# One level of Strassen in the up projections of four feed-forward stages of an eight-block FP32 model

## What is computed

```python
def _swiglu(x, wg, wu, wd):
    return (jax.nn.silu(x @ wg) * (x @ wu)) @ wd
```

## Time and profile before

| what | value |
|---|---|
| time, median of 3 runs | 3176.98 us (3176.74 to 3179.26) |
| the profiled execution's own time | 3175.48 us |
| its span, first to last instruction | 3173.7 us |
| TensorE busy | 3018.4 us, 95% of the span |
| VectorE, ScalarE, GpSimd busy | 1592.3, 1208.5, 527.0 us |
| stage `up3` in the trace | 1909.6 to 2150.3 us |

### The profile page before, as it was taken

How to read it: one execution, slowest core, us unless ns; L and a number is a source line. 1 busy time by engine, 2 the same in 40 slices (tenths; PEclk the granted TensorE clock), 3 DMA queues, 4 the chain that set the end, 5 groups by cost and what they waited for, 6 DMA issues and landing times.

```text
span 3173.7 us, 37430 instructions
## 1 busy us (share of the span) xinstructions
PE 3018.4 (95%) x13606; PEld 2468.7 (78%) x13606; DVE 1592.3 (50%) x1835; ACT 1208.5 (38%) x1599; POOL 527.0 (17%) x517
## 2 busy tenths in 40 slices
PE   7999988889999999799999879999999998999998
PEld 6888876768788887588888668888888886788886
DVE  6665356388566634633337844333433336843323
ACT  5553252258555423422223233222322224732221
POOL 1111010235311111211101111111111102611110
PEclk9999999889999999899999999999999999999999
DMA  4222332100123222222232112322332232222222
GB/s 160 105 93 77 105 124 69 53 14 1 54 93 104 82 91 92 75 105 93 82 103 82 54 40 93 104 86 91 103 101 97 81 104 93 80 93 95 99 84 80
DMA packets 47162, 272.63 MB, mean 86 GB/s; under 512 B 5936, under 2 KB 7776, under 8 KB 24800
## 3 DMA queue, kind: packets, MB, share of 16 engines
q1 hardware_dynamic: 47072, 271.42, 25.0%
HBM read 269.29 MB, written 2.11 MB: 86 GB/s over the span
## 4 chain that ended last, share of the span: by engine, by line
PE 85%; DVE 7%; ACT 3%; issue 2%; POOL 2%; DMA 1%; SPq 0%; POOLq 0%; DVEq 0%; ACTq 0%
PE bank L465 26%; PE bank L467 26%; PE bank L466 26%; PE bank L752 1%; DVE w_lo L1570 1%; ACT probs L1287 1%; POOL sq_sum L2333 1%; PE bank L889 1%; ACT w_hi L1042 1%; PE bank L664 0%; DVE rs L1576 0%; PE bank L478 0%; DVE cy L2034 0%; DVE x L1587 0%; PE bank L768 0%
## 5 line engine op out<-in xcount | busy, mean ns | idle before, releaser
L465 PE MATMUL bank<-h_hi,w_hi 128*128 128x512 f32 x2624 | 1034.3, 394 | 47.2 <-DVE h_lo L1582 24.4
L466 PE MATMUL bank<-h_lo,w_hi 128*128 128x512 f32 x2624 | 1025.0, 391 | 0.0
L467 PE MATMUL bank<-h_hi,w_lo 128*128 128x512 f32 x2624 | 1024.4, 390 | 0.0
L1570 DVE TENSOR_TENSOR w_lo<-w_raw,w_hi 128x2048 fp32r<-128x2048 f32 (+2 forms) x282 | 576.5, 2044 | 580.3 <-ACT w_hi L1042 579.6
L465 PEld LDWEIGHTS bank<-h_hi,w_hi 128*128 128x128 f32 x2624 | 494.5, 188 | 164.6 <-issue 38.5
L1042 ACT ACTIVATE w_hi<-w_raw 128x2048 fp32r<-128x2048 f32 (+2 forms) x282 | 474.8, 1684 | 334.9 <-PE bank L467 306.5
L466 PEld LDWEIGHTS bank<-h_lo,w_hi 128*128 128x128 f32 x2624 | 494.6, 188 | 105.5 <-issue 3.4
L467 PEld LDWEIGHTS bank<-h_hi,w_lo 128*128 128x128 f32 x2624 | 494.5, 188 | 103.8
L465 PE MATMUL bank<-act_hi,w_hi 128*128 128x512 f32 x1056 | 411.7, 390 | 7.3 <-DVE hid L1696 4.7
L467 PE MATMUL bank<-act_hi,w_lo 128*128 128x512 f32 x1056 | 410.9, 389 | 0.0
L466 PE MATMUL bank<-act_lo,w_hi 128*128 128x512 f32 x1056 | 410.8, 389 | 0.0
(11 more groups left out here) (324 smaller groups left out, 2905.1 us busy)
## 6 DMA issues: line engine op xcount, KB each, us to landing
w_raw<-in_w_up SPq DMA_DIRECT2D x132, 1024.0 KB, 4.9
w_raw<-in_w_down SPq DMA_DIRECT2D x96, 704.0 KB, 4.1
w_raw<-in_w_wout SPq DMA_DIRECT2D x12, 1024.0 KB, 4.9
w_raw<-in_w_ple SPq DMA_DIRECT2D x16, 640.0 KB, 3.9
w_raw<-in_w_ein SPq DMA_DIRECT2D x6, 1024.0 KB, 4.9
w_raw<-in_w_kproj SPq DMA_DIRECT2D x4, 1024.0 KB, 5.5
w_raw<-in_w_qproj SPq DMA_DIRECT2D x4, 1024.0 KB, 4.9
w_raw<-in_w_ogate SPq DMA_DIRECT2D x4, 1024.0 KB, 5.0
```

The source lines that it names most:

```text
L465: pe.matmul(out, wh, mh, start=first, stop=False)
L466: pe.matmul(out, wh, ml, start=False, stop=False)
L467: return pe.matmul(out, wl, mh, start=False, stop=final)
L1570: dve.tensor_tensor(w_lo[j % 2][:, 0:n], w_raw[j % 2][:, 0:n], w_hi[j % 2][:, 0:n].bitcast(F32), ALU.subtract).then_inc(w_lo_done, 1)
```

## The change

Stages `up2` to `up5` compute each job's product by one level of Strassen's scheme (in the form with 15 additions). The weights of a job are seen as 2 x 2 blocks: rows are gate (`A11`, `A12`) and value (`A21`, `A22`), columns are the even and the odd chunks of the features. The activations are 2 x 2 blocks as well: even and odd chunks, and left and right 256 tokens. Seven products replace eight. A block product has four chunks of 128 features, three matmuls each, and 256 columns: 84 matmuls of 256 columns for 48 of 512.

- Weight sums, on GpSimd, each of 512 columns: `S1 = A21 + A22`, `S2 = S1 - A11`, `S3 = A11 - A21`, `S4 = A12 - S2`. S3 and S4 are written over A21 and A12 in `w_raw`.
- Seven splits of 512 columns on ScalarE (`fast_hi`) and seven on VectorE (`fast_lo`) stand for one of 2048 on each. Each of the seven blocks has one buffer, so the block of job f + 1 is split when TensorE has used that of job f.
- Partial results are joined by VectorE: `base`, `cross` (two instructions), `top` and `rest` (two), with one copy out of PSUM by ScalarE (`base_copy`).
- The activations' differences are made chunk pair by chunk pair in `prepare_fast` and `split_fast`, where `prepare` and `split_x` were.
- Value columns are no longer scaled with `rs` in front of the product; the result of the down projection is, in PSUM, ahead of its addition to `x`.
- The output projection ahead of `up3` (`even_output`) takes its first two outputs alone and the rest in plain order, where it took them in fours.

TensorE's order in a job is S3, S1, A12, A11 of f + 1, A22, S2 of f + 1, S4. The diff, cut to its core:

```diff
@@ TensorE @@
+            def fast_up(n):
+                def product(w, f, u, chunks=range(4)):
+                    hi, lo = fast_block(w, j0)
...
+                    if chunks[0] == 0:
+                        pe.wait_ge(s_lo, n0 + used_at(w, f))
+                    for c in chunks:
...
+                        pe.matmul(out, hi[:, cols], h[0], start=opens and c == 0, stop=False, skip_group_check=True)
+                        pe.matmul(out, hi[:, cols], h[1], start=False, stop=False, skip_group_check=True)
+                        mm = pe.matmul(out, lo[:, cols], h[0], start=False, stop=c == 3, skip_group_check=True)
...
+                            if not isinstance(i, int) or f >= 2:
+                                pe.wait_ge(s_rest, f0 + f - 1)
+                            product("S3", f, u)
+                            product("S1", f, u)
+                        pe.wait_ge(s_base, f0 + f + 1)
+                        product("A12", f, u)
+                        if more:
+                            if not isinstance(i, int) or f >= 1:
+                                pe.wait_ge(s_top, f0 + f)
+                            product("A11", f + 1, u + 1)
+                        pe.wait_ge(s_cross, c0 + 2 * f + 2)
+                        product("A22", f, u)
+                        if more:
+                            product("S2", f + 1, u + 1)
+                        product("S4", f, u)
...
@@ ScalarE, the loop's body @@
+            def fast_up(n):
+                        if not fixed or f >= 1:
+                            silu(f - 1)
+                        if not fixed or f < NF - 1:
+                            fast_hi(n, "S3", f + 1, u + 1)
+                        if not fixed or f >= 1:
+                            hidden_hi(f - 1)
+                        if not fixed or f < NF - 1:
+                            fast_hi(n, "S1", f + 1, u + 1)
+                            fast_hi(n, "A12", f + 1, u + 1)
+                        if not fixed or f < NF - 2:
+                            fast_hi(n, "A11", f + 2, u + 2)
+                        if not fixed or f < NF - 1:
+                            fast_hi(n, "A22", f + 1, u + 1)
+                            base_copy(f + 1, u + 1)
+                        if not fixed or f < NF - 2:
+                            fast_hi(n, "S2", f + 2, u + 2)
+                        if not fixed or f < NF - 1:
+                            fast_hi(n, "S4", f + 1, u + 1)
...
@@ VectorE, the loop's body @@
+            def fast_up(n):
+                def rest(f, u):
+                    dve.wait_ge(s_mm, w0 + used_at("S4", f))
...
+                    dve.tensor_tensor(z_rest, acc, both, ALU.add).then_inc(s_rest, 1)
+                    dve.wait_ge(s_rest, f0 + f + 1)
+                    dve.tensor_tensor(z_mid, z_mid, rs[:, H2:T], ALU.mult).then_inc(s_right, 1)
...
+                        if not fixed or f >= 1:
+                            rest(f - 1, u + 1)
+                        if more:
+                            fast_lo(n, "S3", f + 1, u + 1)
+                        if not fixed or f >= 1:
+                            hidden(f - 1)
+                            dve.wait_ge(hid_done, n0 + f)
+                            cross(f, u)
+                        if more:
+                            fast_lo(n, "S1", f + 1, u + 1)
+                            fast_lo(n, "A12", f + 1, u + 1)
+                        top(f, u)
+                        if two:
+                            fast_lo(n, "A11", f + 2, u + 2)
+                        if more:
+                            fast_lo(n, "A22", f + 1, u + 1)
+                            base(f + 1, u + 1)
+                        if two:
+                            fast_lo(n, "S2", f + 2, u + 2)
+                        if more:
+                            fast_lo(n, "S4", f + 1, u + 1)
...
@@ GpSimd, the loop's body @@
+            def fast_up(n):
+                def row_minus(f, u):
+                    pool.wait_ge(s_lo, w0 + used_at("A12", f))
+                    fast_sum(n, "S4", f, u)
...
+                        if not fixed or f >= 1:
+                            hidden_lo(f - 1)
+                        if not fixed or f < NF - 1:
+                            row_minus(f + 1, u + 1)
+                        if not fixed or f < NF - 2:
+                            fast_sums(n, f + 2, u + 2)
...
@@ VectorE @@
             def down(n):
+                            if n in FAST:
+                                acc = bank[u // 2][:]
+                                dve.tensor_tensor(acc, acc, rs[:], ALU.mult).then_inc(acc_scaled, 1)
+                                dve.wait_ge(acc_scaled, ND * (n - 2) + m + 1)
                             add_to_x(nxt, m, bank[u // 2][:], factor)
```

More of the change, by code:

```diff
@@ L116 @@
     FREE0[_name] = _at
-    _at += ACC_READS[_name.rstrip("0123456789")]
+    _at += 0 if _name in ("up2", "up3", "up4", "up5") else ACC_READS[_name.rstrip("0123456789")]
 STAGE_ORDER = []
@@ L158, in use_at, with used_at, summed_at @@
     return sum(NT - k for k in USES[x] if k < kb) * P
+def used_at(w, f):
+    if w == "A11":
+        return 7 * f - 1 if not isinstance(f, int) or f else 1
+    if w == "S2":
+        return 7 * f + 1 if not isinstance(f, int) or f else 2
+    last = isinstance(f, int) and f == NF - 1
+    return 7 * f + {"S3": 3, "S1": 4, "A12": 5, "A22": 6 if last else 7, "S4": 7 if last else 9}[w]
+def summed_at(w, f):
+    return 4 * f + {"S1": 1, "S2": 2, "S3": 3, "S4": 4}[w]
 def unit(u):
@@ L172, in pairs @@
 def pairs(eng, n, body, peel=0):
-    if n > 2:
+    if n - peel > 1 and n > 2:
         for i in range(peel):
@@ L210, in build @@
             vcw = sb("vcw", [P, NH, P], F32R, to=part)
+        with ExitStack() as part:
+            t4_lo_b = sb("t4_lo_b", [P, T], F32R, to=part)
         sq = sb("sq", [P, T])
@@ L934, in even_output @@
                 stage = "wout1"
[L935 to L952, removed]
+                j = J0[stage]
+                pe.wait_ge(w_lo_done, j + 1)
+                for part, chunks in enumerate((range(CC, ND), range(CC))):
+                    for n in range(2):
+                        for k in chunks:
+                            if n == 0:
+                                if part == 0:
+                                    pe.wait_ge(ln_lo, k - CC + 1)
+                                else:
+                                    pe.wait_ge(o_lo_done, ND + k + 1)
+                            mm = three(bank[n][:], *tile_of(j % 2, n * ND + k), e_hi[:, k], e_lo[:, k],
+                                       part == 0 and k == CC, part == 1 and k == CC - 1)
+                        if part:
+                            mm.then_inc(seg_done, 1)
+                for q in range(1, 4):
+                    dense(stage, q, e_hi, e_lo, o_lo_done, ND, residual="up3")
             def odd():
@@ L1002, in _ @@
                     pool()
+                elif stage in FAST_STAGES:
+                    fast_up(int(stage[2:]))
                 elif stage.startswith("up"):
@@ L1688, in body @@
                         f = 2 * i + u
[L1689 to L1699, removed]
+                        fixed = isinstance(i, int)
+                        more, two = not fixed or f < NF - 1, not fixed or f < NF - 2
+                        if not fixed or f >= 1:
[19 more added lines that the diff above has]
+                            fast_lo(n, "S4", f + 1, u + 1)
+                        if fixed and f == NF - 2:
+                            dve.wait_ge(s_lo, w0 + 7 * NF)
+                            dve.sem_inc(w_lo_done, NF)
                 pairs(dve, NF // 2, body, peel=1)
+                split_w(j0 + NF)
+                rest(NF - 1, NF - 1)
+                hidden(NF - 1)
             def down(n):
```

346 lines of the change are left out of this document (314 added, 32 removed).

## The result

The changed kernel takes 3513.7 us (median of four runs, 3512.7 to 3517.4), the kernel before 3177.5 us (3176.7 to 3179.3) beside it: a ratio of 1.106, 95% interval 1.105 to 1.108. The predicted time was 3493 us. The profiled execution took 3512.7 us, its span is 3510.8 us for 3173.7: 337.1 us more.

What follows compares the result with a forecast made beforehand. The four stages were taken as bound by TensorE's matmuls before, by the other engines' queue loop after: 3175.5 (profiled execution) + 291 (jobs of 14.25 us) + 25 (starts) = 3491.5, median 3493 us; range 3300 to 3600.

Steps and rivals of the forecast that it cites:

- TensorE's part: Matmuls of up2 to up5: 84 of 256 columns at 0.12 us, 10.1 us a job, giving back 70 us over 88 jobs.
- The loop: Fixed queues of GpSimd, ScalarE and VectorE around one job, without TensorE: closes in 12.5 us, against 10.9 before.
- The meetings: VectorE and GpSimd instructions that both read SBUF twice exclude each other: adds 1.7 us to each job.
- A job: Length of one job in up2 to up5: 14.25 us, 22 to a stage, +291 us over four stages.
- The stages' starts: TensorE standing still at the starts of up2 to up5: +4 to +5 us for three, +10 in up2, sum +25.
- `even_output`: New order of the output projection ahead of up3: the wait behind it was costed at nothing.
- TensorE's idle time: In the four stages: once a job, put down to VectorE's `cross`, 3 to 4 us, with PEclk staying at 1.00.
- the clock falls: Rival, chance 0.08: idle gaps in each job halve TensorE's clock in the four stages; 3937 us, or 3600 and up if partly.
- 4 us is shorter than the stretch that did it: Argument against a clock fall: the expected idle per job is shorter than the 6.9 us that slowed matmuls in the earlier trace.
- GpSimd's waits: Sign in the four stages: GpSimd's only long wait is for A12's low part; waiting most of a job would refute the forecast.
- The other side: Rival, chance 0.11: TensorE stays the bound in the four stages, the loop closing under 10.1 us a job; 3126 us.
- the turn: Job length in the four stages at which the change breaks even, the starts being paid: 10.6 us.

Runs made afterwards that it cites:

- experiment 7: Kernel before with its up2 to up5 matmuls made as two of 256 columns, 96 a job: 3236.9 us, 11.52 us a job.
- experiment 8: Kernel before with 256-column matmuls in up2 to up5, only 84 of 96 a job issued: 3111.1 us, 10.08 us a job.
- experiment 2: Kernel after with VectorE's low parts reading a zeroed PSUM bank as second operand instead of the high part in SBUF: 3364.2 us, 12.43 us a job.
- experiment 1: Kernel after with only the high x high matmul of each three in the four stages, 28 a job instead of 84: 3502.0 us, 14.28 us a job.
- experiment 3: Kernel after with `rest` and `silu` queued ahead of the splits of S2 and S4: 3357.0 us, 1.057 of the kernel before, 12.27 us a job.
- experiment 4: Kernel after with GpSimd's weight sums made for only 2 of each 128 columns: 3218.5 us, 10.8 us a job.
- experiment 5: Kernel after with `rest` and `silu` ahead of the S2 and S4 splits, and low parts reading a zeroed PSUM bank: 3246.2 us, 10.9 us a job.
- experiment 6: Kernel after with `rest` and `silu` ahead of the S2 and S4 splits, and sums on 2 of each 128 columns: 3237.9 us, 10.9 us a job.

## Why the prediction was right, step by step

- **TensorE's part.** Right: 0.12 us a matmul, 10.08 us a job (experiments 7 and 8). The gain of 70 us was 61.5, an eighth smaller.
- **The loop.** Right in its path and its size. Without meetings 12.43 us were measured (experiment 2) for 12.5. TensorE isn't in it (experiment 1), and moving `rest` and `silu` out of it cuts it (experiment 3). The rows of the job give the same pieces: from the end of S2 to the start of `rest` 2.45 us, for 2.46 by my sum; from `rest` to `silu` 1.17, for 1.25.
- **The meetings.** Right in kind: 1.9 us for 1.7. The term mis-sized is that of the sums S1 and S2. I gave them 0.2 each, the lengthening of one sum in the earlier trace rows. From the start of S4 to the end of S2 they took 4.68 us where I had 4.06 + 0.4 = 4.46, since each of the two waits 0.55 for a low part to end, and then needs its 1.15.
- **A job.** 14.36 us for 14.25. Against a distance of 10.88 before that is 88 x 3.48 = 306 us, for +291. Of these 15 us the job's 0.11 makes 10. The rest is a slip of the sum: it took 22 jobs from the stretch of 240.7, which holds 1.3 us besides the 22 x 10.88 = 239.4 of its jobs.
- **The stages' starts.** +22 us inside the stages (328.5 - 306), for +25. up2 has 15.1 of it, for +10; the others 4.0, 0.5 and 2.6, for 4 to 5 each, so the sum is in part luck. In up3 TensorE stood 1.9 us for the last chunk of `x`, just ahead of the stretch, and 2.3 in it for the low part of S1. In up3 the first `hidden` comes 31.6 us behind the stage's first matmul, for 13.0 before. That is 18.6 us more, and 9 of them come back in the stage's last two jobs, which take 11.0 and 8.9 us for 14.36. I had neither term. In experiment 4 the first `hidden` comes after 29.2 us, nearly as late, and only 3 come back. So what the four stages take beyond 88 jobs grew by 42 us in experiment 2, 48 in 3, 50 in 4 and 54 in 5 and 6, and the 25 was right for jobs of 14.36 us only.
- **`even_output`.** Costed at nothing; its TensorE stretch took 47.3 us for 50.0, a gain of 2.8. Not foreseen either were +4.3 and +3.6 us in down3 and down4. Their weights' low parts now come late behind an up stage: inside the stages TensorE waits for `w_lo` 1.8 and 2.2 us (2.6 more stand at the end of up3's stretch). Another 1.7 and 1.6 us are the clock: behind these waits some eight matmuls run 0.43 us apart for 0.227. Outside the four stages it came to +8.6 us, where I had nothing; the other 3.4 of it are spread thin and not traced. With the jobs (+15) and the starts (-3) this makes the 21 us by which 3493 fell short.
- **TensorE's idle time.** `cross`, once a job, as said, but 2.6 us instead of 3 to 4. The step that failed is the clock: I had PEclk at 1.00. It fell to 0.87 to 0.90. In the jobs the slow matmuls only filled part of the gap: a job takes 10.1 us of TensorE at the full level, and the loop left 4.3 us of slack to pay for it. Where TensorE itself is the bound the fall does cost, as the start of down3 shows, behind the last matmul of up3:

```profile
2317.04 0.28 PE L629 MATMUL bank<-h_hi,fb 128*128 128x256 f32 x1
2319.92 0.70 PE L573 MATMUL bank<-act_hi,w_hi 128*128 128x512 f32 x1 [2.60 <-DVE w_lo L1832]
2320.42 0.63 PE L574 MATMUL bank<-act_lo,w_hi 128*128 128x512 f32 x1
2320.85 0.63 PE L575 MATMUL bank<-act_hi,w_lo 128*128 128x512 f32 x1
...
2323.41 0.40 PE L575 MATMUL bank<-act_hi,w_lo 128*128 128x512 f32 x1
2323.65 0.40 PE L573 MATMUL bank<-act_hi,w_hi 128*128 128x512 f32 x1
```

The rival "the clock falls" was right about the fall and wrong about the price; of what I wrote against it, "a fall that fits in the idle time costs nothing" held, and "4 us is shorter than the stretch that did it" did not. The Trainium skill, TensorE: Matmul & The Clock Gate, section "HAM oscillation — how this bites in real kernels", describes this pattern of gaps between bursts; this trace agrees that it comes back in nearly every job. Experiment 1 bounds what it costs in the four stages: they got 17.3 us shorter with two thirds of the matmuls gone.

- **GpSimd's waits.** I wrote that it would have no long wait but the one for A12's low part, and that I was wrong if it waited for most of a job. It waits (120.7 + 32.6) / 21 = 7.3 us of 14.36, just over half, and the longer part is ahead of `hidden_lo`. The sign was badly chosen, not the loop: GpSimd can wait for half a job and its three sums still be a link, since its queue lets it do none of them in the hole.
- **The other side.** It needed the loop under 10.1 us. Sums of 0.49 us bring it to 10.8 only (experiment 4): my 12.5 - 3 x 0.8 = 10.1 forgot that `hidden_lo` still holds up the low part of S1 by 0.77. I put the turn at 10.6 us a job, where starts of 25 us are paid. It lies lower: experiment 4, at 10.76, would be 14 us over the kernel before by that turn, and is 44 over. With what its own stages take beyond their jobs (50 us) and 3 us outside, the turn is near 10.88 - 53 / 88 = 10.3 us (an estimate).

The Trainium skill, SBUF — State Buffer, section "Who interferes with whom", was cited for the lock, and it also says that a VectorE instruction with at most one SBUF input stays clear of GpSimd (outside of modes that these instructions don't use). Experiment 2 agrees: 683 ns beside GpSimd's sums for 1189.

What stays open: whether some order of these queues beats the kernel before. Experiments 5 and 6, which drop the meetings or the sums, end at 10.9 us a job with this order, in the loop through the load. An order that loads earlier, or a third slot for the weights, wasn't tried. Little is to be had: jobs of 10.08 us give back 88 x 0.80 = 70 us, and experiments 2 to 6 lose 42 to 54 us at the stages' ends and 3 to 14 outside the stages, which leaves 2 to 25 us if no order changes these (an estimate).

## What to carry to other kernels

An algorithm that saves TensorE an eighth of its columns hands three other engines more work, and there the sum of the work is not the question: in up3 none of them was busy for more than 76% of the stage (244.65 of 322.44 us), and the stage took a third longer. Follow the fixed queues once around a job, each start from what it waits for, and compare the loop with TensorE's time for the job before building anything. Where VectorE and GpSimd both read two SBUF operands, count 1.70 us for a pair of 512 columns, not the longer of the two, and measure the most that the change could give by itself, as experiment 8 does: here it is a few lines, and it says 1.9%. Then count what each stage loses at its ends: over the four stages of experiments 2 to 6 it is 42 to 54 us.

## What the runs showed of the hardware

- The granted clock fell behind gaps of only 2.7 us: matmuls of 256 columns 0.21 us apart for some 3 us, then 0.12. In the earlier trace rows it was a stretch of 6.9 us. At a stage's start it also fell, in up3 from about 1999.5, behind gaps of 1.9 and 0.34 us, and at the start of down3 behind one of 2.6 us (512 columns 0.43 us apart for 0.227). With a third of the matmuls and the same loop the stretch of up3 had 0.59 in place of 0.88.
- A matmul of 256 columns with weights of its own costs 0.120 us in a stream, 53% of one of 512 (0.227 from 10.88 us for 48).
- VectorE and GpSimd alternate in full: in the job shown the low part ends 0.55 us behind the other's end four times, and the sum 1.15 us behind twice; all four stages have the same figures within 0.03 us.
- A GpSimd sum of 8 columns takes 0.45 to 0.49 us, against 1.29 for 512.
